# A hybrid attention and state-space step: key columns and first projection ahead, squares summed before the ones matmul, output table behind the fourth mask

## The reference

```python
h = rmsnorm(x, g_norm_mix)                  # x * rsqrt(mean(x*x) + eps) * g
z = h @ w_in                                # q 512 | k 128 | v 128 | u 512 columns
a = windowed_attention_with_sinks(q, k, v)  # 128-token window, 8 heads, 2 kv heads
s = ssm(u)                                  # 32 groups, complex state 64, GELU, GLU
x = x + concat(rmsnorm(a), rmsnorm(s)) @ w_out
x = x + hierarchical_moe(rmsnorm(x))        # top-1 of 4 groups, top-2 of 8 experts
y = rmsnorm(x, g_final)
```

## Time and profile before

| | |
|---|---|
| median of 3 runs | 883.07 us (882.0 to 884.96) |
| the profiled execution | 880.52 us, of which the span is 878.8 us |
| busy over the span: TensorE, VectorE, ScalarE, GpSimd | 771.3, 314.2, 213.5, 171.1 us |
| mean granted TensorE clock | 0.936 |
| DMA over the span | 255.78 MB, mean 291 GB/s |

### The profile page before, as it was taken

One profiled execution on the slowest core, in us unless ns is written; L12 is line 12 of the kernel. 1 busy time (PEld: TensorE's weight loads), 2 busy tenths in 40 slices (PEclk: granted clock), 3 DMA queues, 4 the chain that ended last, 5 costly groups with the idle time before them and its releaser, 6 DMA issues.

```text
span 878.8 us, 15294 instructions
## 1 busy us (share of the span) xinstructions
PE 771.3 (88%) x5090; PEld 486.0 (55%) x5091; DVE 314.2 (36%) x766; ACT 213.5 (24%) x448; POOL 171.1 (19%) x380
## 2 busy tenths in 40 slices
PE   5999977799999982999998878888999999999874
PEld 3555556567654552666664444444666666666441
DVE  3899775850234334212221111111222212221216
ACT  4000245400341221122221211212222222222213
POOL 2061005100001002222222212212222222222200
PEclk9999989985889995899998999989999999999997
DMA  8202044180773349699999999999999968999957
GB/s 352 87 0 111 31 57 74 18 231 1 214 327 133 130 188 393 277 419 417 418 414 420 416 421 417 419 420 417 419 411 404 410 274 327 415 419 415 418 219 290
DMA packets 59619, 255.78 MB, mean 291 GB/s; under 512 B 19850, under 2 KB 22794, under 8 KB 36368
## 3 DMA queue, kind: packets, MB, share of 16 engines
q1 hardware_dynamic: 52560, 242.86, 70.5%
q0 software_dynamic: 6240, 11.46, 3.5%
q10 hardware_dynamic: 768, 0.72, 0.2%
HBM read 241.38 MB, written 22.30 MB: 300 GB/s over the span
## 4 chain that ended last, share of the span: by engine, by line
PE 61%; DMA 17%; SPq 9%; DVE 7%; ACT 4%; issue 2%; POOLq 0%; POOL 0%; DVEq 0%; ACTq 0%
PE pair L962 15%; PE pair L984 11%; PE pair L757 8%; DMA slot<-in_w_exp_down 7%; PE pair L620 6%; SPq L338 4%; DMA slot<-in_w_exp_up 3%; PE pair L963 3%; DMA kv_row<-in_w_exp_down 3%; SPq L341 2%; DMA slot<-in_w_in_qkv 2%; PE pair L863 2%; PE pair L682 2%; PE pair L678 2%; PE pair L936 2%
## 5 line engine op out<-in xcount | busy, mean ns | idle before, releaser
L963 PE MATMUL pair<-slot,probs 128*64 128x256 f32 x800 | 178.5, 382 | 0.0
L962 PE MATMUL pair<-slot,probs 128*64 128x256 f32 x576 | 128.9, 382 | 6.7 <-issue 3.3
L1641 DVE TENSOR_TENSOR sums<-iota_t,sums 128x640 bf16<-128x640 f32 x38 | 32.0, 841 | 284.7 <-POOL sums L551 278.6
L984 PE MATMUL pair<-slot,sums 128*64 128x512 f32 x400 | 97.7, 632 | 15.1 <-DMA slot<-in_w_exp_down 11.9
L963 PEld LDWEIGHTS pair<-slot,probs 128*64 128x64 f32 x800 | 109.7, 138 | 0.0
L962 PEld LDWEIGHTS pair<-slot,probs 128*64 128x64 f32 x576 | 79.2, 138 | 46.2 <-issue 13.6
L620 PE MATMUL pair<-reg_h,slot 128*128 128x512 f32 x160 | 82.4, 597 | 4.1 <-DVEq L1282 2.5
L963 PE MATMUL pair<-reg_f,probs 128*64 128x256 f32 x384 | 85.0, 379 | 0.0
L527 POOL DMA_INDIRECT probs<-hf_scr,row_u x38 | 40.1, 1056 | 204.4 <-DMA y_scr<-sums,y_now 112.1
L535 POOL DMA_INDIRECT y_scr<-sums,y_now x40 | 42.8, 1070 | 188.4 <-ACT sums L1196 130.8
L962 PE MATMUL pair<-reg_h,probs 128*64 128x256 f32 x352 | 77.9, 379 | 0.3 <-DMA slot<-in_w_exp_up 0.3
(11 more groups left out here) (378 smaller groups left out, 1102.7 us busy)
## 6 DMA issues: line engine op xcount, KB each, us to landing
slot<-in_w_exp_up SPq DMA_DIRECT2D x22, 2048.0 KB, 24.3
slot<-in_w_exp_down SPq DMA_DIRECT2D x44, 1024.0 KB, 24.4
slot<-in_w_exp_gate SPq DMA_DIRECT2D x16, 2048.0 KB, 27.4
reg_f<-in_w_exp_up SPq DMA_DIRECT2D x10, 2048.0 KB, 25.4
reg_h<-in_w_exp_gate SPq DMA_DIRECT2D x8, 2048.0 KB, 26.8
reg_x<-in_w_exp_gate SPq DMA_DIRECT2D x8, 2048.0 KB, 28.6
reg_h<-in_w_exp_down SPq DMA_DIRECT2D x10, 512.0 KB, 23.1
reg_f<-in_w_exp_down SPq DMA_DIRECT2D x10, 512.0 KB, 21.9
```

The source lines that it names most:

```text
L962: pe.matmul(gu[j][0:TT], lhs, gate_w[g][:, h, c, out], start=n == 0, stop=n == KD - 1)
L963: ins = pe.matmul(gu[j][TT:P], lhs, up_w[q][:, h, c, out], start=n == 0, stop=n == KD - 1)
L984: ins = pe.matmul(yp[TT * h:TT * h + TT], hid_t[:, k, :], down_w[q][k][:, 512 * h:512 * h + 512], start=k == 0, stop=k == KH - 1)
L1641: tt(sel, iota_t[:].unsqueeze(1).to_broadcast([P, NT, P]), place_of[:, 0].unsqueeze(2).to_broadcast([P, NT, P]), ALU.is_equal)
```

## The change

SyncE loads the 128 k columns between the first and the second quarter of x, and the q and the v columns as two transfers after the last quarter. TensorE starts with `project(0)`, quarter by quarter as x is scaled; the sum of the squares is no longer made by 16 matmuls with ones over eight blocks but by VectorE, which adds the blocks together, and two matmuls with ones follow `project(0)`. VectorE empties each projection one place earlier in its list. `out_table(0)` moves from its place ahead of `proj_out(5)` to the end of round 1 (behind `masked(3)`), now with `spare`; `out_table(1)` moves from there to the end of round 2 (behind `masked(4)`).

```diff
         @block.sync
         def _(sp):
+            w_rows = a["w_in_qkv"].rearrange("(p k) n -> p k n", k=KD)
             for h in range(4):
                 kk = slice(2 * h, 2 * h + 2)
                 sp.dma_start(x_t[:, kk, :], a["x_t"][:, kk, :]).then_inc(s[f"in_x{h}"], 16)
-            sp.dma_start(w_qkv, a["w_in_qkv"].rearrange("(p k) n -> p k n", k=KD)).then_inc(s["in_w_qkv"], 16)
+                if h == 0:
+                    sp.dma_start(w_qkv[:, :, W:W + P], w_rows[:, :, W:W + P]).then_inc(s["in_w_k"], 16)
+            sp.dma_start(w_qkv[:, :, 0:W], w_rows[:, :, 0:W]).then_inc(s["in_w_qkv"], 16)
+            sp.dma_start(w_qkv[:, :, W + P:W + 2 * P], w_rows[:, :, W + P:W + 2 * P]).then_inc(s["in_w_qkv"], 16)
...
         def _(pe):
             pe.wait_ge(s["const_done"], 1)
-            for h in range(4):
-                pe.wait_ge(s["sq_done"], h + 1)
-                for k in range(2 * h, 2 * h + 2):
-                    pe.matmul(pp[2][:, 0, :], ones[:], x_sq[:, k, 0:SEQ], start=k == 0, stop=k == KD - 1)
-                    ins = pe.matmul(pp[2][:, 1, 0:P], ones[:], x_sq[:, k, SEQ:TOK], start=k == 0, stop=k == KD - 1)
-            ins.then_inc(s["rstd_ps"], 1)
...
-            pe.wait_ge(s["in_w_qkv"], 16)
-            for n in range(6):
+            pe.wait_ge(s["in_w_k"], 16)
+            project(0)
+            pe.wait_ge(s["sq_sum"], 1)
+            pe.matmul(pp[2][:, 0, :], ones[:], x_sq[:, 0, 0:SEQ], start=True, stop=True)
+            pe.matmul(pp[2][:, 1, 0:P], ones[:], x_sq[:, 0, SEQ:TOK], start=True, stop=True).then_inc(s["rstd_ps"], 1)
+            pe.wait_ge(s["in_w_qkv"], 32)
+            for n in range(1, 6):
                 project(n)
...
                 for k in range(2 * h, 2 * h + 2):
                     ins = ts(x_t[:, k, :], x_t[:, k, :], g_mix[:, k:k + 1], None, ALU.mult)
                 ins.then_inc(s["xg_done"], 1)
+                ins = tt(x_sq[:, 2 * h, :], x_sq[:, 2 * h, :], x_sq[:, 2 * h + 1, :], ALU.add)
+                if h >= 1:
+                    step(ins)
+                    ins = tt(x_sq[:, 0, :], x_sq[:, 0, :], x_sq[:, 2 * h, :], ALU.add)
+                if h < 3:
+                    step(ins)
+            ins.then_inc(s["sq_sum"], 1)
...
+            proj_out(0)
             dve.wait_ge(s["prep_act"], 3)
...
+            proj_out(1)
             power = lambda n: (pw[:, 0, T - n, :], pw[:, 1, T - n, :])
             for n, (x, y) in {2: (1, 1), 3: (2, 1), 4: (2, 2), 5: (4, 1), 6: (4, 2), 7: (4, 3), 8: (4, 4)}.items():
                 cmul(power(n), power(x), power(y), (pv(12), pv(14)))
-                if n == 3:
-                    proj_out(0)
-            proj_out(1)
+            proj_out(2)
...
             dve.sem_inc(s["bbar_done"], 1)
-            proj_out(2)
+            proj_out(3)
...
             step_table(0)
-            proj_out(3)
+            proj_out(4)
             step_table(1)
             dve.sem_inc(s["bp_ready"], 1)
-            proj_out(4)
+            proj_out(5)
...
             dve.wait_ge(s["in_small"], 48)
-            out_table(0, probs[:].rearrange("p b n -> p (b n)"))
-            proj_out(5)
             masked(0)
...
-                if n == 1:
-                    out_table(1, spare)
-                    dve.sem_inc(s["out_tab_done"], 1)
+                if n in (1, 2):
+                    out_table(n - 1, spare)
+                    if n == 2:
+                        dve.sem_inc(s["out_tab_done"], 1)
```

More of the change, by code:

```diff
@@ L236, in build @@
         names = """
-            in_cols in_tables in_small in_x0 in_x1 in_x2 in_x3 in_w_u in_w_qkv in_w_att in_attn in_resid in_rows
+            in_cols in_tables in_small in_x0 in_x1 in_x2 in_x3 in_w_u in_w_k in_w_qkv in_w_att in_attn in_resid in_rows
             out_w
@@ L248, in build @@
             y_copied fin_out fin_sq fin_ms fin_sqrt fin_done sc_read base_step place_ready rows_done
-            pow_ready ffn_ms ffn_sqrt fin_ss diag_done summed""".split()
+            pow_ready ffn_ms ffn_sqrt fin_ss diag_done summed sq_sum""".split()
         names += [f"{n}_in{q}" for n, held in (("gate", 4), ("up", 3), ("down", 3)) for q in range(held)]
```

## The result

The changed kernel takes 887.79 us (median of 20 runs, 885.43 to 890.67) beside 884.92 us (20 runs, 880.83 to 888.6) for the kernel before in the same rounds: a ratio of 1.0042, 95% interval 1.0028 to 1.0056, or 2.5 to 5.0 us slower. The forecast was 1.7 us slower, called no change that can be measured; it is a measurable loss.

A forecast was written before the change was run, and what follows sets the result against it. TensorE and VectorE both run full to about 85 us, and the first bp_copy, behind out_tab_done, sets the change's worth. 2.7 - 1.2 + 0.2 = 1.7 us took 883.07 to 884.8 us; range 881 to 888.

The forecast's parts named there:

- The mechanism: VectorE's full list passes on the row factor's delay; the first bp_copy waits for out_tab_done, 1.5 us later than before.
- r: Delay of the row factor at the front against the kernel before: 2.7 us, bounds 1.0 and 3.5.
- TensorE's seven: TensorE's gain at the front: project(1) starts at 21.4 to 22.3 instead of 29.06, about 7 us earlier.
- the rival in which the table is not felt: At bp_copy: the later out_tab_done holds nothing, TensorE's 7 us reach the end, 876 us; chance 0.10.
- the price of k's load: SyncE's load of k, 512 KB in 512-byte pieces: makes each later quarter of x 1.6 us late.
- TensorE can begin ... at 8.5: Start of project(0): one scaling (1.02 us) behind TensorE's old start of 7.48, at 8.5 us.
- cover: Ahead of kv_rows: TensorE ends near 76, VectorE arrives at 77.9; these 1.9 us hide short waits for copies.
- The rival that named the clock: In project(0): TensorE stays at half pace, r is 9.4, 8.2 us more, 891 us; chance 0.06.
- The additions hidden behind TensorE by 0.5 us: VectorE's sum of squares is ready at 19.7, TensorE's project(0) ends at 20.2: additions hidden by 0.5 us.
- GpSimd's powers: Powers on GpSimd, started by a later signal: VectorE waits between nothing and 1.8 us, taken as 0.2.
- The second table: out_table(1) on VectorE behind masked(4), before the signal bp_copy waits for: another 8.32 us, ending at 128.5.
- late x and late powers: Rival at the front: r 3.5 and the full 1.8 us wait for GpSimd, 4.1 us slower, 887 us; chance 0.14.

The follow-up runs named there:

- e3: Changed kernel with ScalarE's wait for out_tab_done put ahead of copy 5 instead of copy 0: 883.42 us, ratio 0.9984 to the kernel before.
- e5: Changed kernel without VectorE's seven additions of squares (other values, read only up to block 5): row factor at 22.42 us, no ratio.
- e7: Changed kernel with e3's later wait and half of out_table(0) in VectorE's gap ahead of proj_out(8): 881.59 us, ratio 0.9978 to the kernel before.
- e9: Changed kernel with the k columns loaded ahead of the first quarter of x: 889.31 us, ratio 1.0051 to the kernel before.
- e10: Changed kernel with k's 512 KB loaded in 4 KB pieces (other columns and values): row factor at 21.68 us, no ratio.
- e11: Changed kernel with eight unused matmuls added in TensorE's idle stretch ahead of project(7): 888.2 us, ratio 1.0044 to the kernel before.
- e12: Changed kernel with five unused matmuls added in TensorE's idle stretch ahead of project(7): 884.59 us, ratio 1.0011 to the kernel before.
- e4: Changed kernel with the 656 KB of tables loaded on SyncE's queue behind x instead of ScalarE's: 885.39 us, ratio 1.0005 to the kernel before.
- e1: Changed kernel without the move of the output tables (out_table(0) ahead of masked(0), out_table(1) in round 1): 889.21 us, ratio 1.0056 to the kernel before.
- e2: Kernel before with only the two output tables moved: 891.68 us, ratio 1.0076 to the kernel before.
- e8: Kernel before with half of out_table(1) put into VectorE's gap ahead of proj_out(8): 881.14 us, ratio 0.9966 to the kernel before.
- e6: Kernel before with only the order of loads changed, TensorE waiting for k, q and v before project(0): 886.82 us, ratio 1.0027.

## Why the prediction was right or wrong

**The mechanism** held. From the row factor to `kv_rows` VectorE's list takes 56.37 us in the changed kernel and between 56.35 and 56.37 in e3, e5, e7, e9, e10, e11 and e12, whatever TensorE and the loads did; only in e4, where it had to wait 2.2 us for `project(1)`, it was 58.55. In the kernel before it was 64.08. The difference is 7.71 us, the table's 7.73. Every microsecond of r goes through, and of TensorE's seven only what VectorE's shortened list can use comes out: 7.71 less 4.16 at `kv_rows`. The first `bp_copy` then waits for two tables, as forecast; the rival in which the table is not felt fell with that, and e3 shows what it would have needed.

**The step that failed** is the price of k's load: "I take 1.6, as the pieces are alike", bounds 1.3 and 2.04. Measured, the second quarter of x is 3.05 us late (3.1 to 4.2 in the kernels with the same front), and k lands at 10.0 us, 4.8 behind the first quarter. The price was taken from the caches, which came when the tables were long in. As the pace of short pieces that have the engines to themselves it was right: at e4's 302 GB/s 512 KB take 1.7 us, an estimate. It left out what else was loading. Here the tables on the other queue went ahead until 5.5 us, and most of k then fell into a stretch with half idle engines, which the kernel before has under x. e4 and e10 show that the one or the other, short pieces or the tables beside them, must go for k to land at 7.6 us; even that is 2.5 to 2.6 behind the first quarter of those traces. The rule weighed there, that pieces of 512 bytes run at line rate (the Trainium skill, DMA: Bandwidth & Descriptors, Specifications), does not hold here: with the engines fully busy the short pieces came at 302 GB/s, the long ones of the tables at 425.

With it fell "TensorE can begin ... at 8.5": it needs k too, and began at 10.06, 1.56 us later. By the prediction's way the row factor follows 13.0 us behind that start; measured it is 12.94, so that r is 2.7 + 1.56 less 0.1, that is 4.16, past the upper bound of 3.5. That 12.94 meets 13.0 is partly luck. The prediction had TensorE as the last to finish, with VectorE 0.5 us ahead of it; in the trace VectorE is last. Its scaling of the second quarter begins 1.5 us late (13.02 instead of 11.5) and the last quarter's ends at 19.33 instead of 18.0. The five other kernels with this front need 13.05 to 14.02 us, most where the second quarter of x comes last behind TensorE's start (e1, e3). `kv_rows` at 79.37 instead of 77.9 is r and nothing else.

**The cost that was missing** is TensorE's idleness ahead of `project(7)`. The prediction called 1.9 us of it cover and priced it at nothing. With `kv_rows` and the copy of `project(6)` it is 4.78 us, the clock falls to half, and `project(7)` holds VectorE 1.14 us (e12). The rival that named the clock looked for it in the first projection, where TensorE's own gaps were at most 0.2 us and the pace rose as before.

**The terms that held or fell on the other side.** The additions hidden behind TensorE by 0.5 us: they were not, and cost about 0.5 (e5). GpSimd's powers: priced 0.2, no wait was there. The second table: 8.3, measured 8.22. `project(1)` from 21.4 to 22.3: 22.73, at once behind the ones. q and v: no wait, as they landed at 20.6 and 22.3. The gap ahead of `proj_out(8)`: 4.66, unchanged.

The sum for the first `bp_copy` was 1.7 us; with 1.46 more for r, 1.14 for the clock and 0.2 less for the powers it is 4.1, measured 3.95. `turn_bp` at half clock throughout adds 0.43, which makes nearly all of the 4.41 at block 5. The runs are 2.5 to 5.0 us slower; how the delay at block 5 becomes the time of the whole kernel was not followed to the end. The time lies just inside the stated range of 881 to 888, but what was held likeliest, no change (0.63), is not what came: two terms of the sum were too small by 2.6 us together. The rival "late x and late powers" gave nearly the time that was measured, but by half of its reasons: the late x was there, the late powers were not.

## What to carry to other kernels

Before work is taken off one engine, lay the other engines' lists beside it: where two run full, only the shorter saving counts, and a step moved behind the next wait is paid again there (e1, e2). Price a load by the rows of what is loading beside it, not by the same pieces at a quieter time. Before two traces are compared, look whether a stage with the same list ran at the same clock in both: e2 and e8 differ from the kernel before by 1.4 to 1.9 us ahead of their edits. And look for a gap that is already there before making one: half a table in VectorE's 4.66 us (e8) gave more than the whole rearrangement, and a wait put ahead of the first write that needs it (e3) undid the loss with one line.

## What the hardware showed that was not expected

- Pieces of 512 bytes that have the DMA engines to themselves came at 302 GB/s with the engines fully busy (e4, 5.0 to 6.0 us), pieces of 5 KB at 425 (the changed kernel, 4.5 to 5.5 us).
- While k came in pieces of 512 bytes on one queue, the 656 KB on the other landed 2.3 us sooner than before (6.5 instead of 8.8 us) and k 2.4 us later than in 4 KB pieces. Behind the tables the engines were only 0.51 to 0.57 busy, with long pieces in the kernel before and with short ones in the changed kernel; what causes that was not tried.
- A TensorE that is made to finish early can be slower afterwards: 4.78 us without work cost 1.14 us on the next projection. The length of the idle stretch alone does not decide it: ahead of `project(0)` the engine stood idle for 2.05 us in e2 and fell to half pace, and for 2.37 us in e6 and stayed at full pace (first pairs 1.10, 1.02 and 1.02 us). In the other direction, the late block 6 ran at clock 1.00 instead of 0.85 and was 1.5 us shorter; e11, with the same start of block 6, ran at 0.85.
